# 512-column matmuls in conv-in and the first MLP's up units, their two parts added on GpSimd

## The chip, the core and the metric

The kernel runs on one core of a Trainium2 chip. The metric is the device time of one execution in microseconds, the median over several runs. The core has five engines with a queue each: TensorE (PE in the profile, its weight loads PEld), VectorE (DVE), ScalarE (ACT), GpSimd (POOL) and SyncE (SP), whose queue issues nearly all DMAs.

## The reference, cut to what matters

The network has four layers at width 1024 over 256 tokens, all in fp32. Layer one, where the change lies, is

```
mod = silu(c) @ ada_w + ada_b            # six vectors of shift, scale and gate for a layer
h   = modulate(rmsnorm(x), sh1, sc1)
b, c, hv = split(h @ w_in, 3)            # conv-in: 1024 x 3072
y   = (b * conv3(c * hv)) @ w_out        # conv3: causal, three taps, by channel
x   = x + gt1 * y
h   = modulate(rmsnorm(x), sh2, sc2)
x   = x + gt2 * (relu(h @ w1)**2 @ w2)   # first MLP: 1024 x 4096 x 1024
```

The other layers (an RWKV-7 mixer and two attentions, each with an MLP) follow and aren't changed.

## The kernel before, in words

**Units.** All weights stream through SBUF in units of 1 MB: 1024 rows by 256 columns ("dense": conv-in, MLP up), or 512 rows by 512 columns ("wide": conv-out, MLP down). A unit lands by DMA in one of four `stage` buffers. fp32 precision comes from splitting each operand in a high and a low part: ScalarE copies `stage` to `w_hi` in the reduced type (L882, two halves), VectorE subtracts to make `w_lo` (L1507, two halves), both double-buffered by unit number. A product is hi·hi + hi·lo + lo·hi, three matmuls (`three`, L2252 to L2254).

**A dense unit** (`unit`, called at L2465 and L2502). For each of 8 row blocks `kt` and each of two column halves `m`, `three` moves 256 columns (256 tokens) three times: `h_hi`, then `h_lo` against `w_hi`, then `h_hi` against `w_lo`, all summed in one half of one PSUM bank `un[..]`. So 48 matmuls with 48 weight loads. The two banks alternate between units; the third user of a bank waits in `free_bank` until the first result was read.

`h_hi` and `h_lo` lie side by side in `h_both`. The up units of the later MLPs already move both at once (`up_unit`, L2290: 512 columns into a pair of banks; L2293: 256 columns of `h_hi` against `w_lo`), and two engines add the two parts afterwards.

**Conv-in** is 12 dense units: 0 to 3 give `b_gate`, 4 to 7 `tmp`, both copied by ScalarE from PSUM (`evac`, L1044); for units 8 to 11 VectorE multiplies the bank by `tmp` (L1815), makes the three taps (L1818, L1822), the product with `b_gate` (L1826, `zf`), and, after the low part of a later unit, `z_lo` (L1591). ScalarE makes `z_hi` (L1040) when `zf` is there. Conv-out is four wide units that need `z` (two row blocks per `zf`).

**The first MLP** is four groups of four up units and four down units. After an up unit ScalarE makes `relu` from the bank (L1053), VectorE squares it against the bank (L1712, `zf`), then come the low part of the unit after next, `z_lo`, and often a "weigh".

**Weighing.** The layer vectors `mod` need 48 MB of `ada_w`. 28 of its 1 MB pieces are multiplied on VectorE by `silu(c)` in two instructions each (L1786 or L1789), one piece behind each of 28 "slots": conv-in units 0 to 7 (slots 0 to 7), and in the MLP (slot 16 is its first unit) slots 18 to 24, 26 to 38. Set sums, turns and a few products of these run on TensorE between units.

**Order.** Every queue is in program order, written out by hand. ScalarE behind a dense unit: read the bank, split the unit after next, `z_hi`. VectorE behind an MLP up unit: `zf`, low part of the unit after next, `z_lo`, weigh. SP loads unit u+4 when the low part of unit u is made. GpSimd has nothing to do until L746, where it scales the lora weights of the next layer during the MLP's last group.

Quoted from the matmuls of a dense unit:

```
2252  MM(out, hi_l, hi_r, start=start, stop=False, skip_group_check=True)
2253  MM(out, hi_l, lo_r, start=False, stop=False, skip_group_check=True)
2254  return MM(out, lo_l, hi_r, start=False, stop=stop, skip_group_check=True)
```

Of the kernel before, what the change touches and what calls it, by code (L numbers as in the profile page):

```python
# [13 lines left out]
P = 128  # L14
SEQ = 256
# [85 lines left out]
def build(nc, A, out):  # L101

    with ExitStack() as ctx:
# [83 lines left out]
        gate_rows = [at(f"gate_row{i}", [P, D], o) for i, o in enumerate((sq_off + 4096, scr_off + 20 * 1024, sq_off + 4096, r_off[0]))]  # L187
# [15 lines left out]
        relu_b = [at(f"relu{i}", [P, 2, SEQ], scr_off + 16 * 1024 + 2048 * i) for i in range(2)]  # L203
# [256 lines left out]

        ROPE_USE = (0, 1, 2, 3, 5, 6, 7, 8)
# [7 lines left out]
        def freed(v):  # L469

            return v + 1
# [156 lines left out]
        def _(sp):  # L628
# [73 lines left out]
        scaled_made, sq_f_ready, both_ready, square_ready, root_row_done, root_row_out, tables_made = (  # L702
            sem(n) for n in ("scaled_made", "sq_f_ready", "both_ready", "square_ready", "root_row_done", "root_row_out", "tables_made"))
        full_made, h_hi_made, h_lo_made = (sem(n) for n in ("full_made", "h_hi_made", "h_lo_made"))
        zf_ready, z_hi_made, z_lo_made, relu_ready = (sem(n) for n in ("zf_ready", "z_hi_made", "z_lo_made", "relu_ready"))
# [20 lines left out]
        silu_e, silu_ready, rep_ready = sem("silu_e"), sem("silu_ready"), sem("rep_ready")  # L726
# [3 lines left out]
        def _(pool):  # L730
# [11 lines left out]
            pool.wait_ge(sem("lora1_loaded"), 16 * 3)  # L742
            pool.wait_ge(ada_summed, len(WEIGHED_SETS))
            for lo, hi, which in LORA_COLS:
# [121 lines left out]
        def _(act):  # L866
# [178 lines left out]

            def mlp(m, n_next, gain_next=None):
                u, v, zc = U_MLP[m], V_MLP[m], Z_MLP[m]
                for g in range(GROUPS):
                    for j in range(UPD):
                        uu = u + 2 * UPD * g + j  # L1050
                        if m == 0:
                            act.wait_ge(unit_done, uu + 1)
                            A_(relu_b[j % 2][:], un[(v + j) % 2][:], ACT.Relu).then_inc(relu_ready, 1)  # L1053
# [12 lines left out]
                        if m == 0:  # L1066
                            copy_set(COPIED_AT.get(S_MLP + 2 * UPD * g + j))
# [417 lines left out]
        def _(dve):  # L1485
# [218 lines left out]
            def mlp(m, n_next, row, gain_next=None):  # L1704
                u, v, zc = U_MLP[m], V_MLP[m], Z_MLP[m]
                for g in range(GROUPS):
                    for j in range(UPD):
                        uu = u + 2 * UPD * g + j
                        k = zc + UPD * g + j
                        if m == 0:  # L1710
                            dve.wait_ge(relu_ready, UPD * g + j + 1)
                            V.scalar_tensor_tensor(out=zf[k % 2][:], in0=un[(v + j) % 2][:], scalar=0.0, in1=relu_b[j % 2][:],  # L1712
                                                   op0=ALU.max, op1=ALU.mult).then_inc(zf_ready, 1)
                            dve.wait_ge(zf_ready, zf_count(k))
                            V.engine_nop().then_inc(un_free, 1)
# [16 lines left out]
                        if g == 0 and j == 2 and m >= 2:  # L1732
                            both_rms(N_MLP[m], rms)
                            V.tensor_tensor(rms_square, rms, rms, ALU.mult).then_inc(square_ready, 1)
                            dve.wait_ge(square_ready, m - 1)
# [21 lines left out]
            V.tensor_tensor(c_silu, vecT[:, VEC_C:VEC_C + KT], small[:, 24:32], ALU.mult).then_inc(silu_ready, 1)  # L1757
            dve.wait_ge(silu_ready, 1)
# [47 lines left out]
            for j in range(12):  # L1806
# [349 lines left out]
            V.tensor_scalar(sel_bias[:], score[:], 0.5 * TAKEN, NEG, ALU.is_gt, ALU.mult).then_inc(sem("keys_chosen"), 1)  # L2156
            dve.wait_ge(sem("keys_chosen"), 1)
# [89 lines left out]
        def _(pe):  # L2247
# [12 lines left out]
            def unit(u, bank, xs, ready=None, tokens=False, first=True, last=True, kts=range(KT)):  # L2260
# [16 lines left out]
                if kts[-1] == KT - 1:  # L2277
                    ins.then_inc(unit_done, 1)

# [178 lines left out]
            def mlp(m, n):  # L2458
                u, v, zc = U_MLP[m], V_MLP[m], Z_MLP[m]
                for g in range(GROUPS):  # L2460
                    for j in range(UPD):
                        ready = h_ready(n) if g == 0 and j == 0 else None
                        if m == 0:
                            free_bank(v + UPD * g + j)
                            unit(u + 2 * UPD * g + j, un[(v + j) % 2], (h_hi, h_lo), ready)  # L2465
# [45 lines left out]
            keep_warm(V_MLP[0], 3)  # L2511
# [516 lines left out]
```

## Time and profile before

| what | value |
|---|---|
| median of 3 runs | 1351.02 us (1350.86 to 1354.01) |
| span of the profiled execution | 1350.7 us |
| PE busy | 1303.9 us, 97% of the span |
| DVE busy | 948.4 us, 70% |
| ACT busy | 701.1 us, 52% |
| POOL busy | 128.3 us, 9% |
| DMA | 256.9 MB, mean 190 GB/s |

The profiled execution has no time of its own beside its span; the two nearest runs lie 0.2 and 0.3 us above the span, so a sum made against the span can be read against the median. A row of the timeline gives the start, the duration and the engine of an instruction, its line, and, in brackets, how long the engine stood idle before it and who ended that. Matmuls overlap: their durations don't add up, the distance of their starts does. A row of busy time by stretch gives the stretch, its length, the busy us of PE, PEld, DVE, ACT and POOL with their instructions, the granted clock (1.00 is the full 2.4 GHz), the DMA share and GB/s. Conv-in runs from 36 to 112 us, conv-out to 136, the first MLP from 145 to 332.

### The profile page before, as it was taken

How to read it: one execution, taken by the hardware profiler on the slowest of the kernel's cores; microseconds unless marked ns; L12 is line 12 of the kernel's file. 1: busy time of each engine (PE TensorE's matmuls, PEld its weight loads, DVE VectorE, ACT ScalarE, POOL GpSimd, SP SyncE). 2: the span in 40 equal slices, each digit the busy share in tenths (PEclk: the TensorE clock that was granted, in tenths of full speed). 3: DMA queues.
4: the chain of work that ended last, by engine and by line, in shares of the span. 5: the costliest groups of instructions: out<-in, count | busy, mean ns of one | idle time of the engine just before them, and what ended most of it. 6: DMA issues, size and time to landing. Idle time of an engine off the chain costs nothing. (4 is left out here: it accounts for less than half of the span.)

```text
span 1350.7 us, 24951 instructions
## 1 busy us (share of the span) xinstructions
PE 1303.9 (97%) x10507; PEld 1130.7 (84%) x10507; DVE 948.4 (70%) x1433; ACT 701.1 (52%) x1211; POOL 128.3 (9%) x133
## 2 busy tenths in 40 slices
PE   4999999999999999999999999999999999999997
PEld 2998888997899887788888887888888998888886
DVE  1887788976768776685556888666657677756655
ACT  2534544434467455564444648654445566644443
POOL 0000000010200864100000142000000021000000
PEclk9999999999999999999999999999999999999999
DMA  9997899995341012356665532465565544565561
GB/s 363 373 366 236 302 350 381 356 344 161 110 156 64 4 35 97 98 178 196 188 192 177 176 121 74 150 203 192 187 196 160 170 143 126 172 188 192 183 197 51
DMA packets 177559, 256.90 MB, mean 190 GB/s; under 512 B 10472, under 2 KB 122536, under 8 KB 177448
## 3 DMA queue, kind: packets, MB, share of 16 engines
q1 hardware_dynamic: 177448, 255.31, 57.0%
q8 instruction: 83, 1.36, 0.4%
q14 instruction: 28, 0.23, 0.0%
HBM read 254.25 MB, written 1.05 MB: 189 GB/s over the span
## 5 line engine op out<-in xcount | busy, mean ns | idle before, releaser
L1507 DVE TENSOR_TENSOR w_lo<-stage,w_hi 128x1024 fp32r<-128x1024 f32 (+1 forms) x372 | 447.3, 1238 | 160.4 <-ACT w_hi L882 160.0
L882 ACT ACTIVATE w_hi<-stage 128x1024 fp32r<-128x1024 f32 (+1 forms) x378 | 379.9, 1049 | 211.7 <-PE acc L2311 191.9
L2309 PE MATMUL acc<-w_hi,z_hi 128*128 128x512 f32 x640 | 252.7, 395 | 1.6 <-DVE z_lo L1956 1.6
L2311 PE MATMUL acc<-w_hi,z_lo 128*128 128x512 f32 x640 | 249.4, 390 | 0.0
L2310 PE MATMUL acc<-w_lo,z_hi 128*128 128x512 f32 x640 | 249.2, 389 | 0.0
L2252 PE MATMUL un<-h_both,w_hi 128*128 128x256 f32 x736 | 214.9, 292 | 1.8 <-POOL w_lo L853 1.1
L2253 PE MATMUL un<-h_both,w_hi 128*128 128x256 f32 x736 | 208.8, 284 | 0.0
L2254 PE MATMUL un<-h_both,w_lo 128*128 128x256 f32 x736 | 208.8, 284 | 0.0
L2252 PEld LDWEIGHTS un<-h_both,w_hi 128*128 128x128 f32 x736 | 141.6, 192 | 9.5 <-issue 5.4
L2309 PEld LDWEIGHTS acc<-w_hi,z_hi 128*128 128x128 f32 x640 | 120.1, 188 | 27.8 <-issue 3.9
L2253 PEld LDWEIGHTS un<-h_both,w_hi 128*128 128x128 f32 x736 | 141.7, 193 | 1.2 <-issue 0.7
L2254 PEld LDWEIGHTS un<-h_both,w_lo 128*128 128x128 f32 x736 | 141.7, 193 | 0.0
L2311 PEld LDWEIGHTS acc<-w_hi,z_lo 128*128 128x128 f32 x640 | 120.1, 188 | 25.4
L2310 PEld LDWEIGHTS acc<-w_lo,z_hi 128*128 128x128 f32 x640 | 120.2, 188 | 23.4
L2290 PE MATMUL un<-h_both,w_hi 128*128 128x512 f32 x384 | 121.2, 397 | 0.4 <-DVE w_lo L1507 0.4
L2290 PE MATMUL side<-h_both,w_hi 128*128 128x512 f32 x384 | 120.8, 396 | 0.4
L2293 PEld LDWEIGHTS side<-h_both,w_lo 128*128 128x128 f32 x384 | 72.1, 188 | 17.0
L2293 PEld LDWEIGHTS un<-h_both,w_lo 128*128 128x128 f32 x384 | 72.1, 188 | 16.9
L2293 PE MATMUL un<-h_both,w_lo 128*128 128x256 f32 x384 | 75.5, 278 | 0.0
L2293 PE MATMUL side<-h_both,w_lo 128*128 128x256 f32 x384 | 75.5, 278 | 0.0
L1789 DVE SCALAR_TENSOR_TENSOR ada_sum<-ada_buf,small,ada_sum 128x1024 f32<-128x1024 f32 x49 | 62.8, 1282 | 1.0
L2290 PEld LDWEIGHTS un<-h_both,w_hi 128*128 128x128 f32 x384 | 59.1, 189 | 1.7 <-DVE w_lo L1507 0.6
(393 smaller groups left out, 1885.1 us busy)
## 6 DMA issues: line engine op xcount, KB each, us to landing
stage<-in_mlp_w SPq DMA_DIRECT2D x64, 1024.0 KB
ada_buf<-in_ada_w SPq DMA_DIRECT2D x48, 1024.0 KB, 11.1
stage<-in_w_up SPq DMA_DIRECT2D x32, 1024.0 KB
stage<-in_w_down SPq DMA_DIRECT2D x32, 1024.0 KB
stage<-in_conv_w_in SPq DMA_DIRECT2D x12, 1024.0 KB
stage<-in_rw_w_rkv SPq DMA_DIRECT2D x12, 1024.0 KB
stage<-in_w_in_a SPq DMA_DIRECT2D x8, 1024.0 KB
stage<-in_w_kv_b SPq DMA_DIRECT2D x8, 1024.0 KB
```

Source lines behind the costliest of these rows:

```text
L882: A_(w_hi[u % 2][:, half, 0:n], stage[u % NSTAGE][:, half, 0:n], ACT.Copy).then_inc(hi_made, 1)
L1507: V.tensor_tensor(w_lo[u % 2][:, half, 0:n], stage[u % NSTAGE][:, half, 0:n], w_hi[u % 2][:, half, 0:n].bitcast(F32), ALU.subtract).then_i ...
L1789: V.scalar_tensor_tensor(out=to[:], in0=rows, scalar=by, in1=to[:], op0=ALU.mult, op1=ALU.add).then_inc(ada_weighed, 1)
L2252: MM(out, hi_l, hi_r, start=start, stop=False, skip_group_check=True)
L2253: MM(out, hi_l, lo_r, start=False, stop=False, skip_group_check=True)
L2254: return MM(out, lo_l, hi_r, start=False, stop=stop, skip_group_check=True)
L2290: MM(pair[:, m, :, :], wh[:, kt, c], h_both[:, kt, :, :], start=(kt == 0), stop=False, skip_group_check=True)
L2293: ins = MM(pair[:, m, 0, :], wl[:, kt, c], h_hi[:, kt, :], start=False, stop=(kt == KT - 1), skip_group_check=True)
L2309: MM(y, z_hi[:, kt, q], wh[:, i, :], start=(first and kt == 0), stop=False, skip_group_check=True)
L2310: MM(y, z_hi[:, kt, q], wl[:, i, :], start=False, stop=False, skip_group_check=True)
L2311: ins = MM(y, z_lo[:, kt, q], wh[:, i, :], start=False, stop=(last and kt == KT - 1), skip_group_check=True)
```

## The change

Conv-in's 12 units and the first MLP's 16 up units go through a new `half_unit`. For each column half `m` in turn it moves `h_hi` and `h_lo` together (512 columns, hi·hi and hi·lo side by side) and then `h_hi` against `w_lo` into the first 256 columns, 8 row blocks long, into bank `un[m]`. So 32 matmuls and 32 weight loads for 48. ScalarE copies each bank when its half is done (`copy_half`, 512 elements, into `halves[i % 2]`), GpSimd adds the two parts of both halves in one instruction (128x512), and VectorE takes the sum from SBUF. `evac` for conv-in, the MLP's `relu` copy and the extra VectorE wait go away. The next unit's first half waits for the copy of bank 0, its second half for that of bank 1. Moved: GpSimd's lora scaling goes behind the last three adds, the first gate row to another buffer, and the load of the second constant table behind a wait of SP that stood just below it. Some semaphores become chain links.

```diff
+        halves = [at(f"halves{i}", [P, 2, 2, SEQ], sq_off + 4096 * i) for i in range(2)]
...
                 if u == U_MLP[0] + 8:
+                    sp.wait_ge(sem("x_ready"), x_done(N_MLP0))
                     sp.dma_start(const[1][:], A["const_table"][:, CONST_AT[1]:CONST_AT[2]]).then_inc(sem("const_mid_in"), 16)
-                    sp.wait_ge(sem("x_ready"), x_done(N_MLP0))
...
+            for i in range(len(HALF_UNITS)):
+                pool.wait_ge(un_free, freed(half_use(i)))
+                both = halves[i % 2]
+                if i < 8:
+                    to = (b_gate if i < 4 else tmp)[:, 2 * (i % 4):2 * (i % 4) + 2, :]
+                else:
+                    to = both[:, :, 0, :]
+                G.tensor_tensor(to, both[:, :, 0, :], both[:, :, 1, :], ALU.add).then_inc(sum_made, 1)
+                if i >= len(HALF_UNITS) - 3:
+                    lora_scale(*LORA_COLS[i - len(HALF_UNITS)])
...
+            def copy_half(i, m):
+                if m:
+                    act.wait_ge(unit_done, HALF_UNITS[i] + 1)
+                else:
+                    act.wait_ge(half_done, i + 1)
+                if i >= 2:
+                    act.wait_ge(sum_made, i - 1)
+                A_(halves[i % 2][:, m, :, :], un[m][:, :, :], ACT.Copy).then_inc(un_free if m else half_free, 1)
...
                         if m == 0:
-                            act.wait_ge(unit_done, uu + 1)
-                            A_(relu_b[j % 2][:], un[(v + j) % 2][:], ACT.Relu).then_inc(relu_ready, 1)
+                            if j == 0:
+                                copy_half(12 + UPD * g, 0)
+                            copy_half(12 + UPD * g + j, 1)
...
                         if m == 0:
+                            if j < UPD - 1:
+                                copy_half(12 + UPD * g + j + 1, 0)
                             copy_set(COPIED_AT.get(S_MLP + 2 * UPD * g + j))
...
+            copy_half(0, 0)
             for j in range(12):
-                if j < 8:
-                    dst = (b_gate if j < 4 else tmp)[:, 2 * (j % 4):2 * (j % 4) + 2, :]
-                    evac(U_CONV_IN + j, V_CONV + j, dst)
+                copy_half(j, 1)
                 split(U_CONV_IN + j + 2)
                 if j >= 8:
                     z_split(Z_CONV + j - 8, j - 8)
+                if j < 11:
+                    copy_half(j + 1, 0)
...
                         if m == 0:
-                            dve.wait_ge(relu_ready, UPD * g + j + 1)
-                            V.scalar_tensor_tensor(out=zf[k % 2][:], in0=un[(v + j) % 2][:], scalar=0.0, in1=relu_b[j % 2][:],
-                                                   op0=ALU.max, op1=ALU.mult).then_inc(zf_ready, 1)
-                            dve.wait_ge(zf_ready, zf_count(k))
-                            V.engine_nop().then_inc(un_free, 1)
+                            dve.wait_ge(sum_made, 12 + UPD * g + j + 1)
+                            up = halves[j % 2][:, :, 0, :]
+                            V.scalar_tensor_tensor(out=zf[k % 2][:], in0=up, scalar=0.0, in1=up, op0=ALU.max, op1=ALU.mult).then_inc(zf_ready, 1)
...
-                    dve.wait_ge(unit_done, U_CONV_IN + j + 1)
-                    dve.wait_ge(un_free, freed(V_CONV + 7))
-                    V.tensor_tensor(u_pad[:, t0:t0 + 2, 2:PADT], un[(V_CONV + j) % 2][:], tmp[:, t0:t0 + 2, :], ALU.mult).then_inc(un_free, 1)
-                    dve.wait_ge(un_free, freed(V_CONV + j))
+                    dve.wait_ge(sum_made, j + 1)
+                    link(V.tensor_tensor(u_pad[:, t0:t0 + 2, 2:PADT], halves[j % 2][:, :, 0, :], tmp[:, t0:t0 + 2, :], ALU.mult))
...
+            def half_unit(i, ready=None):
+                u = HALF_UNITS[i]
+                wh, wl = w_hi[u % 2], w_lo[u % 2]
+                def rows(kt, m):
+                    c = slice(P * m, P * m + P)
+                    MM(un[m][:, :, :], wh[:, kt, c], h_both[:, kt, :, :], start=(kt == 0), stop=False, skip_group_check=True)
+                    ins = MM(un[m][:, 0, :], wl[:, kt, c], h_hi[:, kt, :], start=False, stop=(kt == KT - 1), skip_group_check=True)
+                    if kt == KT - 1:
+                        ins.then_inc(unit_done if m else half_done, 1)
...
+                if i:
+                    pe.wait_ge(half_free, i)
...
+                for m in range(2):
+                    if m:
+                        pe.wait_ge(un_free, freed(half_use(i) - 1))
+                    for kt in range(together, KT):
...
+                        rows(kt, m)
...
             for j in range(12):
-                free_bank(V_CONV + j)
-                unit(U_CONV_IN + j, un[(V_CONV + j) % 2], (h_hi, h_lo), h_ready(N_CONV) if j == 0 else None)
+                half_unit(j, h_ready(N_CONV) if j == 0 else None)
```

(`together` is 6 where a unit follows the turning of its own input, in the first unit of conv-in and of the MLP, and 0 otherwise.)

## Rows read from the trace of the kernel before

**Rows 1.** The page: span, and busy time of each engine.

```profile
span 1350.7 us, 24951 instructions
PE 1303.9 (97%) x10507; PEld 1130.7 (84%) x10507; DVE 948.4 (70%) x1433; ACT 701.1 (52%) x1211; POOL 128.3 (9%) x133
```

**Rows 2.** Busy time by stretch: conv-in's last units, the MLP's third group of up units.

```profile
90.00:118.70 28.70, 28.70 (x256) 25.15 (x255) 27.03 (x47) 12.07 (x16) 0.00 (x0) 1.00 0.69 244
...
243.50:268.00 24.50, 24.50 (x188) 22.40 (x184) 23.04 (x25) 13.16 (x18) 0.00 (x0) 1.00 0.96 356
```

**Rows 3.** Waits of PE from 35 to 335 us, and of SP's queue.

```profile
PE un L2252 <- DVE w_lo L1507: 0.3, 1, 0.3
...
SPq L637 <- DVE w_lo L1507: 276.5, 53, 17.7
```

**Rows 4.** Timeline of PE inside a conv-in unit: two hi·hi matmuls, one triple apart.

```profile
43.41 0.28 PE L2252 MATMUL un<-h_both,w_hi 128*128 128x256 f32 x1
...
43.77 0.28 PE L2252 MATMUL un<-h_both,w_hi 128*128 128x256 f32 x1
```

**Rows 5.** Timeline of PE in the second MLP: four up units begin and end.

```profile
620.51 0.62 PE L2290 MATMUL un<-h_both,w_hi 128*128 128x512 f32 x2
...
642.79 0.40 PE L2309 MATMUL acc<-w_hi,z_hi 128*128 128x512 f32 x1
```

**Rows 6.** Timeline of POOL and of DVE where GpSimd scales the lora weights.

```profile
291.02 1.04 POOL L746 TENSOR_TENSOR lora_mu<-lora,vecT 128x512 f32<-128x512 f32 x1 [290.58 <-PE side L2436]
...
292.03 2.02 POOL L746 TENSOR_TENSOR lora_mu<-lora,vecT 128x512 f32<-128x512 f32 x1
...
291.89 1.26 DVE L1507 TENSOR_TENSOR w_lo<-stage,w_hi 128x1024 fp32r<-128x1024 f32 x1 [0.26 <-ACT w_hi L882]
...
293.07 2.06 DVE L1507 TENSOR_TENSOR w_lo<-stage,w_hi 128x1024 fp32r<-128x1024 f32 x1
```

**Rows 7.** GpSimd's instructions on two 128x512 tensors, by group, and one alone.

```profile
L783 POOL TENSOR_TENSOR rw<-rw,rw 128x512 f32<-128x512 f32 x4 | 5.9, 1484 | 0.1
...
L761 POOL TENSOR_TENSOR b_fm<-rw,w_inv 128x512 f32<-128x512 f32 x3 | 3.8, 1274 | 0.2 <-PE un L2642 0.2
...
453.38 2.11 POOL L783 TENSOR_TENSOR rw<-rw,rw 128x512 f32<-128x512 f32 x1
```

**Rows 8.** Timeline of DVE and of ACT in conv-in's first eight units.

```profile
52.50 2.60 DVE L1789 SCALAR_TENSOR_TENSOR ada_sum<-ada_buf,small,ada_sum 128x1024 f32<-128x1024 f32 x2
55.98 1.23 DVE L1507 TENSOR_TENSOR w_lo<-stage,w_hi 128x1024 fp32r<-128x1024 f32 x1 [0.88 <-ACT w_hi L882]
...
84.17 0.60 ACT L1044 ACTIVATE tmp<-un 128x512 f32<-128x512 f32 x1 [3.48 <-PE un L2254]
```

**Rows 9.** Conv-in's last four units: ACT behind unit 8, DVE's chain, PE's second conv-out unit.

```profile
89.99 2.01 ACT L882 ACTIVATE w_hi<-stage 128x1024 fp32r<-128x1024 f32 x2 [3.33 <-PE un L2254]
...
90.74 0.69 DVE L1815 TENSOR_TENSOR u_pad<-un,tmp 128x512 f32<-128x512 f32 x1
...
97.43 0.68 DVE L1815 TENSOR_TENSOR u_pad<-un,tmp 128x512 f32<-128x512 f32 x1
...
118.05 0.68 DVE L1591 TENSOR_TENSOR z_lo<-zf,z_hi 128x512 fp32r<-128x512 f32 x1
...
119.47 0.48 PE L2309 MATMUL acc<-w_hi,z_hi 128*128 128x512 f32 x1
```

**Rows 10.** The MLP's third group: DVE behind its last two up units, PE's second down unit.

```profile
256.96 0.68 DVE L1712 SCALAR_TENSOR_TENSOR zf<-un,relu 128x512 f32<-128x512 f32 x1
...
263.27 0.69 DVE L1712 SCALAR_TENSOR_TENSOR zf<-un,relu 128x512 f32<-128x512 f32 x1
264.00 1.22 DVE L1507 TENSOR_TENSOR w_lo<-stage,w_hi 128x1024 fp32r<-128x1024 f32 x1
...
267.65 0.50 PE L2309 MATMUL acc<-w_hi,z_hi 128*128 128x512 f32 x1
```

**Rows 11.** The MLP's second group: DVE behind its third up unit.

```profile
209.83 0.69 DVE L1712 SCALAR_TENSOR_TENSOR zf<-un,relu 128x512 f32<-128x512 f32 x1 [1.71 <-ACT relu L1053]
```

More of the change, by code:

```diff
@@ L186, in build @@
         gated_f = at("gated_f", [P, 2, HALF], tmp_off + 4096)
-        gate_rows = [at(f"gate_row{i}", [P, D], o) for i, o in enumerate((sq_off + 4096, scr_off + 20 * 1024, sq_off + 4096, r_off[0]))]
+        gate_rows = [at(f"gate_row{i}", [P, D], o) for i, o in enumerate((const_off[1], scr_off + 20 * 1024, sq_off + 4096, r_off[0]))]
         final_row, out_row = at("final_row", [P, D], r_off[0] + 4096), at("out_row", [P, D], r_off[0])
@@ L459, in h_lows, with half_use @@
             return t + 1
+        HALF_UNITS = [*range(U_CONV_IN, U_CONV_IN + 12), *(U_MLP[0] + 2 * UPD * g + j for g in range(GROUPS) for j in range(UPD))]
+        def half_use(i):
+            return V_CONV + i
         ROPE_USE = (0, 1, 2, 3, 5, 6, 7, 8)
@@ L701, in build @@
         row_done, row_out, out_made, final_made = (sem(n) for n in ("row_done", "row_out", "out_made", "final_made"))
-        scaled_made, sq_f_ready, both_ready, square_ready, root_row_done, root_row_out, tables_made = (
-            sem(n) for n in ("scaled_made", "sq_f_ready", "both_ready", "square_ready", "root_row_done", "root_row_out", "tables_made"))
+        scaled_made, sq_f_ready, both_ready, root_row_done, root_row_out, tables_made = (
+            sem(n) for n in ("scaled_made", "sq_f_ready", "both_ready", "root_row_done", "root_row_out", "tables_made"))
         full_made, h_hi_made, h_lo_made = (sem(n) for n in ("full_made", "h_hi_made", "h_lo_made"))
-        zf_ready, z_hi_made, z_lo_made, relu_ready = (sem(n) for n in ("zf_ready", "z_hi_made", "z_lo_made", "relu_ready"))
+        zf_ready, z_hi_made, z_lo_made = (sem(n) for n in ("zf_ready", "z_hi_made", "z_lo_made"))
+        half_done, half_free, sum_made = (sem(n) for n in ("half_done", "half_free", "sum_made"))
         lora1_scaled, lora1_done, lora1_out, lora1_turned, lora2_done, lora2_out = (
@@ L739, in link, with lora_scale @@
                 pool.wait_ge(chain, count[0])
-            pool.wait_ge(sem("lora1_loaded"), 16 * 3)
-            pool.wait_ge(ada_summed, len(WEIGHED_SETS))
-            for lo, hi, which in LORA_COLS:
+            def lora_scale(lo, hi, which):
+                pool.wait_ge(sem("lora1_loaded"), 16 * 3)
+                pool.wait_ge(ada_summed, len(WEIGHED_SETS))
                 mu = vecT[:, VEC_MU + 8 * which:VEC_MU + 8 * which + 8].unsqueeze(2).to_broadcast([P, KT, hi - lo])
                 G.tensor_tensor(lora1_mu[:, :, lo:hi], lora1[:, :, lo:hi], mu, ALU.mult).then_inc(lora1_scaled, 1)
+            for i in range(len(HALF_UNITS)):
[8 more added lines that the diff above has]
+                    lora_scale(*LORA_COLS[i - len(HALF_UNITS)])
             for m in range(KT):
@@ L2278, in unit, with low_parts @@
                     ins.then_inc(unit_done, 1)
+            def half_unit(i, ready=None):
[7 more added lines that the diff above has]
+                        ins.then_inc(unit_done if m else half_done, 1)
+                def low_parts(kt):
+                    if kt % (KT // 2) == 0:
+                        pe.wait_ge(lo_made, 2 * u + kt // (KT // 2) + 1)
+                together = KT - 2 if ready is not None else 0
+                if i:
+                    pe.wait_ge(half_free, i)
+                if together:
+                    pe.wait_ge(un_free, freed(half_use(i) - 1))
+                for kt in range(together):
+                    low_parts(kt)
+                    ready(kt)
+                    for m in range(2):
+                        rows(kt, m)
+                for m in range(2):
+                    if m:
+                        pe.wait_ge(un_free, freed(half_use(i) - 1))
+                    for kt in range(together, KT):
+                        if m == 0:
+                            low_parts(kt)
+                            if ready is not None:
+                                ready(kt)
+                        rows(kt, m)
             def up_unit(u, pair, ready=None):
@@ L2463, in mlp @@
                         if m == 0:
-                            free_bank(v + UPD * g + j)
-                            unit(u + 2 * UPD * g + j, un[(v + j) % 2], (h_hi, h_lo), ready)
+                            half_unit(12 + UPD * g + j, ready)
                             ada_piece(S_MLP + 2 * UPD * g + j)
@@ L2510, in _ @@
                 ada_products(k)
-            keep_warm(V_MLP[0], 3)
+            pe.wait_ge(un_free, freed(V_MLP[0] - 1))
+            unread(un[V_MLP[0] % 2], 3)
             turn_first(N_MLP0)
```

12 lines of the change are left out of this document (4 added, 8 removed).

## The prediction

> **What bounds the kernel now.** I read the page first: PE is busy for 97% of the span and no other engine comes near [rows 1], so PE's stream sets the time as long as nobody holds it up. Then busy time by stretch, where the change lies: in both stretches PE is full at the full clock, but VectorE is nearly full too, 27.0 of 28.7 us in conv-in's last units and 23.0 of 24.5 in the MLP's third group of up units; ScalarE is at half, GpSimd does nothing [rows 2]. Then the waits: from 35 to 335 us the longest wait of a dense unit's matmul is 0.3 us, and SP waits 276 us for `stage` buffers to come free, so loads are early and DMA is not the limit [rows 3]. So a shorter matmul stream is worth its full length there, until VectorE's work ends last. That is the question here, since the change gives VectorE a neighbour.
>
> **What PE saves.** Durations of matmuls overlap (0.28 us each), so I take distances of starts. A triple in conv-in takes 43.77 - 43.41 = 0.36 us, three times 0.12 [rows 4]; a unit's 16 triples take 5.76. The later MLPs show the new form: four up units from 620.51 to 642.79, 22.28 us, 5.57 a unit, 0.348 for a 512 and a 256 [rows 5]. The new unit takes the two in alternation where those take two and two; nothing in the rows makes that dearer. Saved: 0.19 a unit, by 28 units 5.3 us, of which conv-in has 2.3 and the MLP 3.0. No more: what the 512-column matmul saves is one weight load of three, and loads already run beside matmuls.
>
> **What ScalarE pays.** 56 bank copies replace 8 `evac` and 16 `relu`, at 0.60 each [rows 8]: 19 us more, in stretches where it is half idle. Its order costs more than its time, below.
>
> **What GpSimd costs.** 28 adds of two 128x512 tensors; such an instruction takes 1.27 us undisturbed, 1.48 on average in another place, 2.1 at worst [rows 7]. The sum of a unit is ready one copy, one add and about 0.2 of hand-overs (an estimate) after its last matmul: 0.60 + 1.27 + 0.2 = 2.1 us, where `relu` was ready after 0.7. The add itself lies beside other work, but it takes time from VectorE. At 292.03 an instruction that alone took 1.04 took 2.02, beside a running `w_lo`; the next `w_lo`, issued at 293.07, took 2.06 for some 1.22 [rows 6, 10]. So they take turns: each stands still while the other runs, and VectorE lost 0.84 to an instruction of 1.04, its length less 0.2. An add of 1.27 would cost a busy VectorE 1.07, an idle one nothing: 0 and 2.1 are the bounds, I take 1.07.
>
> The Trainium skill says this as a rule (SBUF — State Buffer, Who interferes with whom): a VectorE instruction with two SBUF inputs and a GpSimd instruction that reads SBUF share a port, and the second blocks for the whole length of the first. By that rule the price is 1.27, and the changed `zf` and `u_pad`, which now read SBUF alone, fall under it; the sum below would come out at +0.7 us instead of -0.7.
>
> **Conv-in's first eight units.** VectorE works 4.88 of 5.76 us and idles 0.88 [rows 8]. The add comes 0.7 us behind the unit's end, about when that idle time is, so most of it costs nothing; the rest makes VectorE a little late, with `w_lo` wanted a whole unit later. No stall.
>
> **Conv-in's last four units.** Unit 8 ends at 89.9; VectorE starts on it at 90.74 and then needs 97.43 - 90.74 = 6.69 us a unit, more than PE, so it falls behind and its last `z_lo` ends at 118.7 [rows 9]. PE wants that six matmuls of 0.23 into its second conv-out unit, at 119.47 + 1.4 = 120.9: cover 2.2 us. After: unit 8 ends nine units' savings earlier, 88.2. Its sum is ready 2.1 to 3.4 later, the upper end if the add waits for half of a weigh (2.60 for two, [rows 8]); I take 2.6, so VectorE starts at 90.8, no earlier than before. Four times 6.69 and three adds that meet a busy VectorE, 3.2, end `z_lo` at 120.8. PE would be there at 120.9 - 12 x 0.19 = 118.6 and waits 2.2 us. So conv-in's saving of 2.3 is given back. Between a start 0.5 earlier and one 0.8 later, the stretch ends 0.6 earlier to 0.7 later than before.
>
> **The MLP.** In the first and fourth group VectorE has little or no weighing and keeps up. In the second it stood idle 1.71 us before its third unit [rows 11], which takes up the 1.4 by which the sum comes later; I charge 0.3 for the last add there. The third group weighs behind each up unit: 263.27 - 256.96 = 6.31 us a unit [rows 10] against PE's 5.57. The `w_lo` half for the second down unit ended at 265.2 and was wanted at 267.65 [rows 10], cover 2.4. After, it comes 1.4 (sum for `relu`) and three adds of 1.07 later, less about 1 us for idle gaps and for the wait behind `zf` that goes (an estimate): 3.6; PE comes 0.76 earlier. Stall 3.6 + 0.76 - 2.4 = 2.0. The MLP gains 3.0 - 2.3 = 0.7.
>
> **Moves with one answer.** SP's constant table load goes behind a wait on something made before the MLP began, four units earlier in SP's order: nothing. SP's loads follow `w_lo` and the weighing; both come some us later, against waits of 5 us a load on average [rows 3]: nothing. The lora scaling runs behind the last adds, where nothing is weighed, and is wanted after the down units: nothing. Chain links for semaphores: nothing.
>
> **Sum.** -5.3 + 2.3 + 2.3 = -0.7 us. The span is 1350.7, the median 1351.0; from the median 1350.3. With the price of an add between 0.8 and 1.3 and the start between its ends this gives 1348.6 to 1352.6.
>
> **Rivals.**
> 1. *The adds fall where VectorE idles or reads PSUM, and cost it nothing.* For: in conv-in's first units idle time and add coincide. Against: the stretches of [rows 2] have 6% idle time, and [rows 6] show the turn-taking on `w_lo`, VectorE's commonest instruction. Then only the later sum counts, within the covers of 2.2 and 2.4 but for some 0.4 of conv-out: -4.9, 1346.1.
> 2. *Slower: VectorE becomes the bound, and ScalarE's order hands that to PE.* `z_hi` waits for `zf` and stands ahead of the copy of the next unit's first half, without which PE may not start the unit after. Sum at 2.1, `zf` 0.7, two copies 1.2: 4.0 behind the unit's end, wanted at 5.57. From a lag of 1.5 us on PE goes at VectorE's pace. It decides where an add costs so much that the first eight units don't fit either: 5.57 - 4.88 = 0.7 beside cover of some 3 us over the eight, so above 1.1. At 1.5, the mean of the one group [rows 7], those eight lose 8 x 0.81 - 2.9 = 3.6, and ten adds elsewhere 0.43 each, 4.3: +7.2, 1358. Against: the idle 0.88 takes part of each add.
> 3. *The change does not shorten a unit:* alternating 512 and 256 columns, or the wait in the middle of a unit, costs the 0.012 of each pair. Nothing is saved and, with PE later, less is given back, some 2 to 3 us: 1353.5. Against: [rows 5].
>
> **How the numbers follow.** Forecast 0.58, rival one 0.20, two 0.14, three 0.08. About 0.3%, 4.05 us, is what a measurement of this kernel can tell from no change: the bounds are 1347.0 and 1355.1. Faster: nearly all of rival one and a little of the forecast's low end, 0.21. Slower: rival two and a little of the third, 0.14. Same: 0.65. The range takes in rival one (1345.7) and most of the third (1354.2), and leaves out the second: 1345.7 to 1354.2.
>
> **What would show it.** A changed profile should have pairs of matmuls 0.348 apart; POOL with 28 adds, many longer than 1.27; VectorE's `w_lo`, weigh and conv instructions longer where an add runs; PE waiting about 2 us for `w_lo` or `z_lo` in the second conv-out unit and again around the third group's first two down units, and nowhere else for more than 0.5. No such waits and a time near 1346 would make the turn-taking wrong; waits on `half_free` in unit after unit would be rival two; starts 0.36 apart rival three.

## The result, and the profile after

The changed kernel takes **1357.8 us** (median of 4 runs, 1357.37 to 1358.29) against 1350.9 for the kernel before (median of 4, 1350.80 to 1354.01): the ratio on record is 1.0042, with a 95% interval of 1.0028 to 1.0057 (that of the two medians is 1.0051). So it is slower, by more than can be mistaken for no change; the forecast was 1350.3, its range 1345.7 to 1354.2. A run's time moves with its mean granted clock: the kernel before ran from 1350.4 (0.999) to 1354.7 (0.996) over the study, and all four runs of the changed kernel had 0.996. Each ratio below is against the runs of before on the same chip.

The page of the changed kernel, span and busy time (against [rows 1]):

```profile
span 1356.1 us, 24151 instructions
PE 1304.1 (96%) x10059; PEld 1106.9 (82%) x10059; DVE 957.4 (71%) x1433; ACT 719.6 (53%) x1243; POOL 169.1 (12%) x161
```

PE issues 448 matmuls less and is busy as long as before (1304.1 against 1303.9 us); nearly all of the 5.4 us by which the span grew is time without work for it. Busy time in the stretches of [rows 2]:

```profile
90.00:118.70 28.70, 26.83 (x200) 21.27 (x200) 25.56 (x42) 13.76 (x21) 5.93 (x4) 1.00 0.68 241
243.50:268.00 24.50, 24.33 (x139) 20.30 (x138) 21.14 (x20) 13.54 (x20) 7.36 (x4) 1.00 0.96 362
```

PE, full before, now idles 1.9 us in conv-in's end, and VectorE idles more too (25.56 us busy against 27.03): each waits for the other. PE's waits from 30 to 340 us (who waits <- for whom: total, times, longest), where [rows 3] had nothing over 0.3 for a unit:

```profile
PE side L2506 <- DVE mod L1796: 2.3, 2, 2.0
PE side L2486 <- ACT ada_row L1127: 1.9, 1, 1.9
PE acc L2369 <- DVE w_lo L1538: 1.1, 2, 1.0
PE side L2409 <- DVE mod L1796: 0.9, 1, 0.9
...
PE un L2311 <- DVE w_lo L1538: 0.4, 1, 0.4
```

The two largest are not for the dense units' operands. They are for `ada_row` (a `copy_set` on ScalarE) and for `mod` (an `add_set` on VectorE), small steps of the conditioning that stand in the same queues. Their place in the timeline of PE, ACT and DVE:

```profile
105.01 1.93 PE L2486 MATMUL side<-ada_buf,c_rep 128*32 128x256 f32 x32 [1.87 <-ACT ada_row L1127]
122.50 0.41 PE L2506 MATMUL side<-const,ada_row 128*128 128x128 f32 x2 [1.97 <-DVE mod L1796]
...
103.48 0.63 ACT L1057 ACTIVATE z_hi<-zf 128x512 fp32r<-128x512 f32 x1 [4.29 <-DVE zf L1851]
104.02 0.58 ACT L1071 ACTIVATE halves<-un 128x512 f32<-128x512 f32 x1
104.49 0.38 ACT L1127 ACTIVATE ada_row<-side 128x256 f32<-128x256 f32 x1
...
105.71 0.62 ACT L1071 ACTIVATE halves<-un 128x512 f32<-128x512 f32 x1
...
105.63 0.69 DVE L1622 TENSOR_TENSOR z_lo<-zf,z_hi 128x512 fp32r<-128x512 f32 x1
107.73 0.69 DVE L1841 TENSOR_TENSOR u_pad<-halves,tmp 128x512 f32<-128x512 f32 x1 [1.41 <-POOL halves L761]
...
121.60 0.68 DVE L1622 TENSOR_TENSOR z_lo<-zf,z_hi 128x512 fp32r<-128x512 f32 x1
122.20 0.16 DVE L1796 TENSOR_TENSOR mod<-side,vecT 128x8 f32<-128x8 f32 x1
```

This reads as a circle. ScalarE stands 4.29 us before `z_hi`, since VectorE's `zf` is late; behind `z_hi` stand the copy of unit 10's first half, `ada_row`, two gate-row copies and the copy of its second half, which starts at 105.71 though the unit's last matmul started at 102.86. VectorE in turn waits 1.41 us for that unit's sum. And `mod` follows VectorE's last `z_lo`. In the kernel before, the same two steps had this much room (ACT and PE, then DVE and PE):

```profile
101.90 0.37 ACT L1097 ACTIVATE ada_row<-side 128x256 f32<-128x256 f32 x1
...
103.88 0.64 PE L2426 MATMUL side<-ada_buf,c_rep 128*32 128x256 f32 x8
...
118.65 0.16 DVE L1769 TENSOR_TENSOR mod<-side,vecT 128x8 f32<-128x8 f32 x1
...
119.33 0.38 PE L2446 MATMUL side<-const,ada_row 128*128 128x128 f32 x2
```

The copy ended 103.88 - 102.27 = 1.6 us ahead of PE, and `mod` 119.33 - 118.81 = 0.5 us ahead. The second is the tightest place of the stretch, and the prediction has neither. Last, the granted clock (the column ahead of the DMA share) by stretches of 2 us:

```profile
120.00:122.00 2.00, 0.53 (x3) 0.11 (x1) 2.00 (x3) 1.72 (x4) 0.00 (x0) 1.00 0.00 0
122.00:124.00 2.00, 1.50 (x7) 1.28 (x8) 1.97 (x4) 0.64 (x1) 0.00 (x0) 0.86 0.45 100
124.00:126.00 2.00, 2.00 (x6) 1.54 (x5) 0.75 (x1) 0.00 (x0) 0.00 (x0) 0.50 1.00 330
126.00:128.00 2.00, 2.00 (x8) 1.60 (x7) 0.00 (x0) 0.00 (x0) 0.00 (x0) 0.79 1.04 324
```

Behind PE's idle stretch the clock falls to 1.2 GHz and matmuls come 0.43 us apart instead of 0.23.

**Where the time went**, by the start of the same matmul in each profiled execution, in us against the kernel before (its own start in the second column):

| | before | after | e_pairs | e_port | e_late | e_add8b | e_order | e_pod |
|---|---|---|---|---|---|---|---|---|
| first unit | 35.83 | +0.19 | +0.04 | +0.09 | +0.06 | +0.12 | -0.17 | -0.19 |
| behind ten units | 95.58 | -0.61 | -1.46 | +0.08 | -1.56 | -1.21 | -1.45 | -1.68 |
| products behind unit 10 | 103.88 | +1.13 | +0.81 | +1.00 | -0.62 | -1.41 | -0.66 | -1.85 |
| second conv-out unit | 119.47 | +3.20 | +3.89 | +3.03 | +1.03 | -1.01 | +0.41 | -1.87 |
| conv-out done | 135.99 | +4.81 | +3.92 | +3.05 | +1.06 | -1.01 | +0.87 | -1.41 |
| second group's down units | 214.68 | +3.98 | +2.69 | +3.04 | -0.11 | -2.17 | -0.24 | -2.73 |
| fourth group's up units | 284.36 | +5.42 | +4.13 | +3.04 | -0.68 | -2.74 | +1.36 | -3.13 |
| MLP done | 332.04 | +6.18 | +4.65 | +3.04 | +0.16 | -3.08 | +2.09 | -3.42 |

So the changed kernel is ahead until unit 10, loses 1.7 at `ada_row`, 2.1 at `mod` and 1.6 to the clock, gains 0.8 in the MLP's first two groups and loses 2.2 in its last two. A second fall of the clock, at 344 to 350 us, adds 1.7 behind that. In the next layer's mixer, near 484 us, the changed kernel gains 1.0: the kernel before stands 1.5 us there, the changed one 0.6 (why was not traced). The kernel before then loses 1.5 to a fall of its own at 814 to 820 us, which the changed one does not have. 6.2 + 1.7 - 1.0 - 1.5 = 5.4, the distance of the spans. The medians lie further apart, 6.9, because the profiled execution of before took longer than its median run: where runs of before have both time and span, they lie 1.8 us above their spans, so that its span of 1350.7 belongs to a run of some 1352.5 us (an estimate), and not to the median, beside which it is set ahead of the prediction.

### The profile page after: what moved, and what is told of

It reads as the page before. It is cut to its first block and busy times, and to the rows that moved or that the text cites. A ratio compares the mean times of both kernels' runs of the same rounds, so it can differ in the third digit from the quotient of the medians.

```text
span 1356.1 us, 24151 instructions
## 1 busy us (share of the span) xinstructions
PE 1304.1 (96%) x10059; PEld 1106.9 (82%) x10059; DVE 957.4 (71%) x1433; ACT 719.6 (53%) x1243; POOL 169.1 (12%) x161
## 5 line engine op out<-in xcount | busy, mean ns | idle before, releaser
L2311 PE MATMUL un<-h_both,w_hi 128*128 128x512 f32 x448 | 161.1, 402 | 0.5 <-DVE w_lo L1538 0.4
L2350 PE MATMUL un<-h_both,w_hi 128*128 128x512 f32 x384 | 121.2, 397 | 0.3 <-DVE w_lo L1538 0.3
L2350 PE MATMUL side<-h_both,w_hi 128*128 128x512 f32 x384 | 120.8, 396 | 0.4
L2311 PEld LDWEIGHTS un<-h_both,w_hi 128*128 128x128 f32 x448 | 84.1, 188 | 23.2 <-issue 2.1
L2276 PE MATMUL un<-h_both,w_hi 128*128 128x256 f32 x288 | 85.6, 297 | 1.4 <-POOL w_lo L870 1.1
L2353 PEld LDWEIGHTS un<-h_both,w_lo 128*128 128x128 f32 x384 | 72.1, 188 | 16.9
L2312 PEld LDWEIGHTS un<-h_both,w_lo 128*128 128x128 f32 x448 | 84.7, 189 | 0.1
L2277 PE MATMUL un<-h_both,w_hi 128*128 128x256 f32 x288 | 81.4, 283 | 0.0
```

Source lines behind the costliest of these rows:

```text
L2311: MM(un[m][:, :, :], wh[:, kt, c], h_both[:, kt, :, :], start=(kt == 0), stop=False, skip_group_check=True)
L2312: ins = MM(un[m][:, 0, :], wl[:, kt, c], h_hi[:, kt, :], start=False, stop=(kt == KT - 1), skip_group_check=True)
L2350: MM(pair[:, m, :, :], wh[:, kt, c], h_both[:, kt, :, :], start=(kt == 0), stop=False, skip_group_check=True)
L2353: ins = MM(pair[:, m, 0, :], wl[:, kt, c], h_hi[:, kt, :], start=False, stop=(kt == KT - 1), skip_group_check=True)
```

## The experiments

Theory A: an add costs VectorE time through the turn-taking of [rows 6], and the sum comes later; VectorE's lateness is handed to PE by queues that keep their order, and a fall of the clock follows. Against it stand the MLP as the cause (B), something behind the changed stretch (C), ScalarE's copies (D), PE's alternating matmuls (E), a VectorE that is simply full (F).

**One half of the change alone.** Conv-in's units changed and the MLP's as before:

```diff
-HALF_UNITS = [*range(U_CONV_IN, U_CONV_IN + 12), *(U_MLP[0] + ...)]
+HALF_UNITS = [*range(U_CONV_IN, U_CONV_IN + 12)]
```

> Only conv-in's twelve units are changed; the first MLP's up units, their relu and zf are as before. Theory A (the late sums of conv-in reach PE through ScalarE's and VectorE's fixed order, and a clock drop behind it): nearly all of the loss is here, conv-out ends some 4.8 us later than before, 1355 to 1357 us. Rival B (the loss comes from the MLP's third group, where the forecast put 2 us): conv-out ends at most 1 us later and the time is 1350 to 1352. Rival C (the loss lies behind the changed stretch and shows up however little is changed): about 1357 here and with the MLP alone.

1355.96 us, ratio 1.0031 (1.0020 to 1.0042); conv-out ends 5.39 later than before, of which 0.79 was there at the first unit, and the MLP then adds nothing. And the MLP's units alone:

```diff
-HALF_UNITS = [*range(U_CONV_IN, U_CONV_IN + 12), *(U_MLP[0] + ...)]
+HALF_UNITS = [*(U_MLP[0] + ...)]
```

> Only the first MLP's sixteen up units are changed; conv-in's units and their evictions are as before. Theory A: the MLP alone adds what it added in the changed kernel, its end 1.0 to 1.5 us later than before at most, 1350.5 to 1352.5 us; waits for w_lo of about 1 us in the second down unit of the third group and nothing near 120 us. Rival B: 1355 to 1357. Rival C: about 1357.

1354.99 us, ratio 1.0020 (1.0012 to 1.0029), above what A gave (1350.5 to 1352.5). Its trace is as A has it: the MLP starts 0.26 earlier and ends 0.93 later than before, a loss of 1.2, with waits for `w_lo` and `mod`. The rest of its 3.6 over that call's before (1351.42) is only in part accounted for: its profile has the clock at half at 464 to 466 us, where before had none, and its runs lie 2.0 us above their spans against 1.8. So both halves lose, conv-in most, so B falls as the main cause; C falls, since the loss is seen at the places themselves.

**PE's order.** The unit takes its row blocks two and two:

```diff
-for m in range(2):
-    rows(kt, m)
+for m in range(2):
+    high_row(kt, m)
...
+for m in range(2):
+    low_row(kt, m)
```

> The changed kernel with one edit: a unit takes its 512- and 256-column matmuls two and two, as the later MLPs do, in place of alternating. Theory A: starts 0.348 us apart per pair instead of 0.3535, so PE's units are 0.09 us shorter each; where PE waits for VectorE the gain is lost again (conv-in and the third group), 1355.5 to 1357.5 us. Rival E (the alternation costs more than its 0.0055 a pair): 1352 to 1355.

1356.96 us, ratio 1.0040 (1.0028 to 1.0053). The same three up units, from their first matmul to the first down matmul, in the changed kernel and here:

```profile
201.61 0.48 PE L2311 MATMUL un<-h_both,w_hi 128*128 128x512 f32 x1
...
218.66 0.40 PE L2369 MATMUL acc<-w_hi,z_hi 128*128 128x512 f32 x1
```

```profile
200.56 0.70 PE L2311 MATMUL un<-h_both,w_hi 128*128 128x512 f32 x2
...
217.37 0.40 PE L2377 MATMUL acc<-w_hi,z_hi 128*128 128x512 f32 x1
```

17.05 and 16.81 us, where the kernel before needs 214.68 - 197.32 = 17.36: a unit saves 0.10 in the changed kernel and 0.18 two and two. But alternation has two paces. In e_order (below), whose units alternate as the changed kernel's do, the same three units need 214.44 - 197.71 = 16.73 us, which saves 0.21 a unit:

```profile
197.71 0.48 PE L2318 MATMUL un<-h_both,w_hi 128*128 128x512 f32 x1
...
214.44 0.39 PE L2376 MATMUL acc<-w_hi,z_hi 128*128 128x512 f32 x1
```

An alternating pair lies either 0.354 or 0.347 from the next, for a whole unit or several; two and two, pairs lie 0.348 to 0.349 apart in all 28 units. In the changed kernel's profile 24 of 28 units have the slower pace, in e_order 12 and in e_late (below) 15 have the faster one. What sets it was not found, so the 0.10 is what the changed kernel got in this execution and not the price of the order. The table shows that the gain of two and two lasts where VectorE keeps up: 0.85 us ahead of the changed kernel behind ten units, 0.3 behind `ada_row`, 1.5 at the MLP's end. The time is in the range of A, and E explains at most a smaller gain, not a loss.

**Adds that cost next to nothing.** This leaves out most of the sum:

```diff
-G.tensor_tensor(to, both[:, :, 0, :], both[:, :, 1, :], ALU.add)
+G.tensor_tensor(to[:, :, 0:8], both[:, :, 0, 0:8], both[:, :, 1, 0:8], ALU.add)
```

> Leaves out most of the sum: GpSimd adds 8 of the 256 columns of the two parts, the rest of the low part is dropped (b_gate is filled with ones once). PE, ScalarE and every wait stay as in the changed kernel. Theory A (the length of the adds does it: sums come later, and time is taken from VectorE's two-input instructions): the waits for ada_row, mod and w_lo and the clock drop in conv-out go, what is left is PE's shorter stream and what lies behind: 1348 to 1351 us. Rival D (the bank copies and ScalarE's order do it, not the adds): the waits stay, 1355 to 1358. Rival C (it lies behind the changed stretch): conv-out and the MLP end no later than before, and yet 1353 or more.

1348.71 us, ratio 0.9977 (0.9967 to 0.9986). The waits for `ada_row` and `w_lo` are down to 0.3 and less, those for `mod` to 0.4, and no fall of the clock is left in the first 340 us; the MLP ends 3.08 earlier than before. All copies and queues are as in the changed kernel, so D falls: it is the adds.

**Only the turn-taking.** The kernel before with 28 spare adds that nobody uses:

```diff
+for i in range(12):
+    pool.wait_ge(un_free, freed(V_CONV + i))
+    link(G.tensor_tensor(spare[:, :, 0, :], spare[:, :, 0, :], spare[:, :, 1, :], ALU.add))
...
```

> The kernel before, to which GpSimd adds 28 spare 128x512 adds on a tile of their own, each let go when the unit's bank is evicted or relu is made; nobody waits for them in either stretch (the const table and the first gate row lie where the changed kernel has them, and two fills of the spare tile go with it). Theory A1 (the time taken from VectorE is what costs): three or four adds of 1.07 against a cover of 2.2 us at conv-out and three against 2.4 in the third group: PE waits 1 to 2 us and 0.5 to 1 us, 1352.5 to 1356 us. Theory A2 (the late sums cost it, and the time taken from VectorE is covered): within 0.7 of before, 1350.7 to 1352. That VectorE loses nothing: z_lo, w_lo and weigh as long as before.

1355.20 us, ratio 1.0025 (1.0015 to 1.0034). The timeline of DVE and POOL in conv-in's last units:

```profile
98.87 0.68 DVE L1828 TENSOR_TENSOR u_pad<-un,tmp 128x512 f32<-128x512 f32 x1
99.59 1.65 DVE L1831 TENSOR_SCALAR conv_y<-u_pad,vecT 128x256 f32<-128x256 f32 x2
...
106.59 0.68 DVE L1828 TENSOR_TENSOR u_pad<-un,tmp 128x512 f32<-128x512 f32 x1
...
99.69 1.39 POOL L747 TENSOR_TENSOR spare<-spare 128x512 f32<-128x512 f32 x1 [6.33 <-DVE u_pad L1828]
```

And PE's waits from 30 to 340 us:

```profile
PE side L2461 <- DVE mod L1782: 2.2, 2, 1.8
...
PE side L2441 <- ACT ada_row L1110: 0.9, 1, 0.9
```

A unit takes VectorE 106.59 - 98.87 = 7.72 us where it took 6.69 [rows 9]: an add costs 1.03, against 1.07 forecast. PE loses 3.0 at exactly the two places, though its own instructions are those of the kernel before. In the MLP, where A1 expected waits of 0.5 to 1, the same adds cost nothing: there the cover holds them.

**Only the lateness.** GpSimd fills the tile twice, which reads nothing, and then adds 8 columns (the rest of the sum is left out):

```diff
+link(G.memset(to, 1.0))
+link(G.memset(to, 1.0))
+G.tensor_tensor(to[:, :, 0:8], both[:, :, 0, 0:8], both[:, :, 1, 0:8], ALU.add)
```

> Leaves out the sum as the run with 8 columns does, but lets GpSimd fill the sum's tile twice first (two fills of 128x512, some 0.5 us each, which read nothing), so that the sum comes about as late as in the changed kernel while VectorE's two reads meet no reader. Theory A with both parts (time taken from VectorE and late sums add up): between the run with 8 columns and the changed kernel; conv-out ends 1 to 3 us later than with 8 columns, the MLP's third and fourth groups wait 1 to 2 us; 1350 to 1353 us. Theory A1 (only the time taken from VectorE costs): within 0.5 of the 8 columns, 1348 to 1349.5. Theory A2 (only the lateness costs): 1356 or more.

1352.18 us, ratio 1.0001 (0.9991 to 1.0010), between the two as A with both parts has it. VectorE's instructions keep their lengths (`z_lo` 0.69), but the wait for the late sum is there:

```profile
106.08 0.69 DVE L1843 TENSOR_TENSOR u_pad<-halves,tmp 128x512 f32<-128x512 f32 x1 [1.51 <-POOL halves L763]
```

The table now splits the loss from the 8 columns to the changed kernel. Conv-in and conv-out: 1.06 + 1.01 = 2.1 by late sums, 3.20 - 1.06 = 2.1 by turn-taking, 1.6 by the clock. The MLP alone: 1.2 by late sums and 2.3 by turn-taking. This split is rough, to about 1 us: the executions also differ in their matmuls' pace (behind ten units e_late is 0.95 ahead of the changed kernel, and in the MLP its faster units make some 0.5 of the 2.3, an estimate from their starts). Nor do the two parts simply add up: turn-taking without late sums, e_port, costs 3.0 in conv-in and nothing in the MLP.

**The order.** `copy_set` and the copies of the next unit ahead of `z_hi`, and the last unit's `add_set` ahead of its product:

```diff
+copy_set(COPIED_AT.get(S_CONV + j))
+copy_half(j + 1, 0)
+copy_half(j + 1, 1)
 z_split(Z_CONV + j - 8, j - 8)
...
+add_set(ADDED_AT.get(S_CONV + j))   # DVE, j == 11
 dve.wait_ge(sum_made, j + 1)
```

> The changed kernel with its order mended in conv-in's last four units: on ScalarE copy_set and the copies of the next unit's two banks stand ahead of z_hi, on VectorE the last unit's add_set stands ahead of that unit's product. Theory A (the in-order queues hand VectorE's lateness to PE, and wait on each other: a copy behind z_hi behind zf behind a sum behind a copy): PE's wait for ada_row (1.9) goes, VectorE's idle 1.4 before the third product goes, the wait for mod becomes at most 0.7 for z_lo, and the clock drop at 124 us goes with it: conv-out ends 4 to 5 us earlier than in the changed kernel, 1352.5 to 1354 us. Rival F (VectorE is simply the bound there, order only renames the wait): z_lo ends as late and conv-out at most 1.8 us earlier, 1356 to 1357.5.

1353.78 us, ratio 1.0014 (1.0005 to 1.0024): some 4 us better than the changed kernel, and conv-out ends 3.9 earlier. Of this, 0.8 was there behind ten units already (the pace of the matmuls, the start of the first unit); 3.1 is left to the order, with the fall of the clock that goes with it. The adds are all still there and as dear; what is left in this stretch are mainly waits for `w_lo` of 0.8 and 0.9. So F, that order only renames the wait and brings at most 1.8, falls.

**The clock.** Unread matmuls in PE's wait for `mod`:

```diff
+if slot == 12:
+    unread(un[0], 8)
 if slot in TURNED_AT:
     turn_set(TURNED_AT[slot])
```

> The changed kernel with eight unread 512-column matmuls on un[0] ahead of the turn of slot 12, in the time in which PE waits for mod. They take nothing from the path (1.8 us of the 2.0 that PE waits). Theory A: the clock drop at 124 us follows from PE's idle stretch, so it goes and conv-out ends 1.6 us earlier, 1355.5 to 1356.5 us. Rival G (the drop comes for another reason, or moves elsewhere): as the changed kernel or up to 1 later, 1357 to 1359.

1362.11 us, ratio 1.0075 (1.0060 to 1.0090): mis-sized, and still of use. The timeline of PE, and then busy time and clock:

```profile
120.16 7.03 PE L2416 MATMUL un<-const 128*128 128x512 f32 x16
```

```profile
122.00:124.00 2.00, 2.00 (x6) 0.83 (x5) 1.97 (x4) 0.42 (x1) 0.00 (x0) 1.00 0.62 115
124.00:126.00 2.00, 2.00 (x6) 0.95 (x5) 0.58 (x1) 0.00 (x0) 0.00 (x0) 1.00 1.02 336
```

Each unread matmul is two records 0.43 apart, so eight held PE for 6.9 us instead of 1.8. But the clock stays full, and conv-out loses nothing after its second unit starts (+7.70 and +7.70), where the changed kernel lost 4.81 - 3.20 = 1.61. That is the price of this fall. With two:

> As the earlier run with unread matmuls, but two in place of eight: each took 0.86 us there, so two fit into the 2.0 us that PE waits for mod. Theory A (the clock falls behind PE's idle stretch and costs 1.6): granted clock 1.0 from 120 to 130 us, conv-out ends 3.1 to 3.4 us later than before instead of 4.8, 1355.5 to 1357 us. Rival G (two don't keep it up, or the drop comes elsewhere): a stretch at half within the next 30 us, 1357 to 1359.

1356.62 us, ratio 1.0033 (1.0024 to 1.0043). The stretch from 120 to 136 is at full clock, and the time is in the range expected; but in the profiled run the fall had come earlier, behind the wait for `ada_row`:

```profile
104.00:106.00 2.00, 0.97 (x12) 0.61 (x16) 2.00 (x3) 2.00 (x6) 0.00 (x0) 0.72 0.44 176
106.00:108.00 2.00, 2.00 (x25) 1.00 (x20) 0.60 (x2) 2.00 (x3) 1.28 (x1) 0.50 0.43 89
```

So conv-out ended 4.38 later than before, not 3.1 to 3.4: the fall is not tied to one place.

**Half units only where there is room.** Conv-in's first eight and the MLP's first two groups, two and two, and then with the order mended too:

```diff
+NC, NG = 8, 2
+HALF_UNITS = [*range(U_CONV_IN, U_CONV_IN + NC), *(U_MLP[0] + 2 * UPD * g + j for g in range(NG) ...)]
```

> The new unit, two and two, only where VectorE has room by the runs so far: conv-in's first eight units and the MLP's first two groups, 16 units; the other 12 units as before. Theory A (a half unit gains 0.19 wherever VectorE keeps up, and costs only where it doesn't): conv-out ends 0.5 to 1.2 us earlier than before, bounded by the wait for mod, the MLP gains another 1.2 to 1.5, no wait of PE over 0.7: 1348.5 to 1350 us, 0.3 of it outside the span. Rival (a half unit costs wherever it stands, since the adds also delay the w_lo and weigh of these stretches): 1351 to 1354.

1349.98 us, ratio 0.9990 (0.9981 to 0.9998).

> As the run with 16 half units, and with the order mended in conv-in's last four units: copy_set ahead of z_hi on ScalarE, the last unit's add_set ahead of its product on VectorE. Theory A (what bounds conv-out after a gain is add_set, which stands behind z_lo and is wanted 1.4 us ahead of it): conv-out ends another 0.3 to 0.8 us earlier, 1348.0 to 1349.5 us. Rival (the order matters only when VectorE is late by more than this): the same as without it within 0.2.

1350.93 us, ratio 0.9992 (0.9984 to 1.0001). Both end the MLP earlier than before (1.13 and 1.68). The MLP's two groups bring 1.2 as expected; conv-in's eight units don't bring their 0.5 to 1.2 (conv-out is done 0.10 later and 0.45 earlier, with first units 0.27 later and 0.33 earlier): the first old unit needs both banks empty, a wait of 0.7, and `mod` takes 0.3 to 0.4. The mended order moves no time that these runs can tell, as its rival had it.

**The adds on VectorE**, all 28 units, two and two, order mended:

```diff
-G.tensor_tensor(to, both[:, :, 0, :], both[:, :, 1, :], ALU.add).then_inc(sum_made, 1)
+V.tensor_tensor(to, both[:, :, 0, :], both[:, :, 1, :], ALU.add).then_inc(sum_made, 1)
```

> All 28 half units, two and two, order mended in conv-in's last four units, and the adds on VectorE in place of GpSimd. Theory A (an add of 0.65 on VectorE is cheaper than 1.03 through the port, and the sum is ready earlier): conv-out ends 0.3 to 1.2 us earlier than before, the MLP's third and fourth groups wait 1 to 2 us in all, 1349 to 1351 us. Rival (VectorE's own time is what is short, whoever takes it: 28 adds of 0.65 are 18 us more work): PE waits for w_lo and z_lo as with GpSimd's adds, 1352 to 1355.

**1348.71 us**, ratio 0.9973 (0.9964 to 0.9983): faster than both kernels, with nothing left out, and a little below what A gave (1349 to 1351): conv-out ends 1.41 earlier, and no up or down unit of the MLP waits over 0.4, where A had 1 to 2 us of waits. An add in the timeline of DVE, and then the two stretches:

```profile
111.71 0.68 DVE L1829 TENSOR_TENSOR halves<-halves 128x512 f32<-128x512 f32 x1
112.31 0.16 DVE L1793 TENSOR_TENSOR mod<-side,vecT 128x8 f32<-128x8 f32 x1
```

```profile
90.00:118.70 28.70, 28.70 (x209) 22.78 (x208) 28.00 (x49) 15.06 (x23) 0.00 (x0) 1.00 0.67 241
243.50:268.00 24.50, 24.48 (x133) 20.07 (x132) 24.22 (x28) 13.45 (x20) 0.00 (x0) 1.00 0.93 334
```

VectorE is busy 28.00 of 28.7 us (27.03 in the kernel before), and PE is full again. An add takes 0.60 of its queue here, against 1.03 when GpSimd made it. Against e_order two things differ, the engine of the adds and the order of the matmuls, and no run has the one without the other. The MLP ends 2.09 + 3.42 = 5.5 us earlier; two and two is worth at most 28 x 0.09 = 2.5 of it (an estimate from the units above), so that some 3 are left to the engine.

## Why the prediction was wrong

**Right:** the price of an add (1.07; measured 1.03, and 1.10 where `z_lo` took 1.79 instead of 0.69). By the Trainium skill (SBUF — State Buffer, Who interferes with whom) the engine that comes second stands until the first one's instruction is over. The prediction took the rule to mean a loss of the add's whole length, which would be 1.4 for the spare adds; but VectorE loses only what is left of an add that already runs. In e_port the add ran from 99.69 to 101.08, and the second of the two VectorE instructions in the row at 99.59 started at 99.85 and ended at 101.24, so the trace agrees with the rule. VectorE's last `z_lo` was forecast at 120.8 and ended at 122.3. In between lie a unit 8 that ended some 1 us later (its last copy started at 89.42; forecast 88.2), since PE had saved less, and the wait of 1.41 in place of one of the three turns. Conv-in's first eight units cost nothing, as forecast. SP's waits of 276 us in [rows 3] are those from 0 to 335 us; from 35 us on they are 203.5 in 44 waits, which changes nothing in the argument. The third group was charged 2.0 of waits: from its first up unit (3.97 later than before) to the fourth group's it lost 5.42 - 3.97 = 1.45 with 0.4 saved, 1.9.

**The step that failed** is the cover in conv-in's last four units: "PE wants that six matmuls of 0.23 into its second conv-out unit ... cover 2.2 us". `z_lo` was not the next thing wanted from that queue. `add_set` stands behind it, and PE wants its `mod` at 119.33, 1.6 us before it wants `z_lo`: cover 0.5. And `copy_set` stands on ScalarE behind `z_hi`, cover 1.6. The prediction counted the instructions of the chain that it had in mind, and not all that stand in its queues and have a reader. In place of a wait of 2.2 that gives back a saving of 2.3 there were waits of 1.9 and 2.0. e_port shows both (0.9 and 1.8) with nothing else changed for PE, and e_order takes most of them away. Behind the second wait the clock fell, which cost another 1.6.

**PE's saving** was a mis-sized term: 0.19 a unit by [rows 5], "nothing in the rows makes that dearer". In the changed kernel's profile 24 of 28 units went at the slower pace of alternation and saved 0.10, some 24 x 0.09 = 2.2 us less in all (an estimate). The order that [rows 5] show, e_pairs, has the 0.18 in every unit; alternation at its faster pace had 0.21.

**The clock** was not in the sum: 1.6 in conv-out, shown by e_warm, and 1.7 behind the MLP (against 1.5 in before's profile, at another place).

**The MLP's fourth group** was to keep up. It lost 0.8 where 0.4 was saved: `row_of_columns` waits 0.9 for `mod`, again an `add_set` behind a `z_lo`. Second group: 0.3 charged, none lost. So the MLP, forecast at -0.7, came out at +1.4.

**The rivals.** Rival two has the time, 1358, and the half of its mechanism that is ScalarE's order; but its way was through late copies in conv-in's first eight units, which it had lose 3.6 us. They lost none, so its number is right by chance. Rival three has about half of its effect in the changed kernel's profile, by a pace that the same order did not keep in other runs. Rival one's cause, adds that cost nothing, is e_add8b: 3.1 us earlier by the end of the MLP.

What stays open: why the clock falls behind some of PE's idle stretches and not behind others, what sets the pace of alternating matmuls, and the 0.3 us that the changed kernel's runs lie further above their spans than before's (2.1 against 1.8; 1.8 with the adds on VectorE).

## What to carry to other kernels

When an engine is made later, list everything in its queue that another engine reads, small steps too, with the time at which each is wanted: the least cover counts, not that of the large operand. An add on an idle engine is not free if it takes turns with a busy one: here 0.60 on VectorE itself was cheaper than 1.03 through GpSimd, and the sum came sooner. And a wait of PE can cost more than its length, since the clock may fall behind it.

## What was not expected of the hardware

A VectorE instruction with one tensor to read also waits for GpSimd: `TENSOR_SCALAR` on 128x256, 0.62 for two, took 1.65 beside a spare add. The rows of the prediction showed turn-taking for `w_lo`, which reads two. The Trainium skill has it (SBUF — State Buffer, Who interferes with whom): `tensor_scalar` is among the operations that can take both ports, and these rows agree.

512- and 256-column matmuls in alternation take 17.05 us (changed kernel) or 16.73 (e_order) for three units, two and two 16.81, with the same matmuls.

The granted clock fell to 0.5 behind waits of PE of 2.0 (mod, 122 us), 2.1 and 2.3 us (`ada_row`, 104 us, in e_warm2 and e_pairs). It did not behind waits of 1.9 (`ada_row` in the changed kernel) and 1.8 (`mod` in e_port). But the length of a wait does not decide it. The fall at 344 to 350 us in the changed kernel came behind waits of 1.06 and 1.00, and the one at 814 to 820 in the kernel before behind one of 1.06 (PE's last row ahead of the fall, and the clock):

```profile
345.02 0.42 PE L2379 MATMUL acc<-const,xs_rw 128*128 128x128 f32 x2 [1.00 <-DVE sq L1888]
346.00:348.00 2.00, 2.00 (x5) 1.40 (x5) 1.93 (x6) 0.69 (x2) 1.19 (x2) 0.50 0.88 296
```

```profile
814.31 0.36 PE L2252 MATMUL un<-h_both,w_hi 128*128 128x256 f32 x1 [1.06 <-POOL w_lo L853]
816.00:818.00 2.00, 2.00 (x11) 2.00 (x10) 1.48 (x3) 0.00 (x0) 2.00 (x3) 0.50 0.00 0
```

The same two waits as at 344, 1.06 and 0.99 at 336 to 339 us in the kernel before, were followed by no fall.
